# The order of VectorE's work per expert tile in a dense expert stage, and of the first tile loads on the SyncE queue

## What is computed

```python
def peer_ffn(x, w_q, sub_keys, u_tab, v_tab):
    ...
    best_s, pos = lax.top_k(cand_s, PEER_TOPK)
    expert = jnp.take_along_axis(cand_i, pos, axis=-1)
    gate = jax.nn.softmax(best_s, axis=-1).astype(x.dtype)
    ...
    def eval_block(args):
        xc, ec, gc = args
        u = u_tab[ec]
        act = jax.nn.gelu(jnp.einsum('cd,chkd->chk', xc, u), approximate=False)
        return jnp.einsum('chk,chkd->cd', act * gc, v_tab[ec])
```

## Time and profile before

| | |
|---|---|
| median of 3 runs | 1670.76 us (1669.7 to 1673.65) |
| the profiled execution | 1677.62 us, its span 1675.4 us |
| PE busy | 1625.1 us, 97% of the span |
| DVE busy | 1323.9 us, 79% |
| ACT, POOL busy | 703.8 us (42%), 594.1 us (35%) |
| first dense iteration | 864 us from the span's start |
| change from n < 64 to n >= 64 | about 1397 us |

### The profile page before, as it was taken

The page is one execution under the profiler, slowest core; times in us unless marked ns, Lnnn a source line. Parts: engine busy times, 40 slices in busy tenths (PEclk is TensorE's granted clock), DMA queues, the critical chain, the costliest instruction groups (busy, mean ns, idle before and its releaser), DMA issues.

```text
span 1675.4 us, 28110 instructions
## 1 busy us (share of the span) xinstructions
PE 1625.1 (97%) x10843; PEld 1440.7 (86%) x10843; DVE 1323.9 (79%) x2700; ACT 703.8 (42%) x1065; POOL 594.1 (35%) x400
## 2 busy tenths in 40 slices
PE   8999999999999997999999999999999999999997
PEld 7876579887889997999999999989989898788886
DVE  5657676883999998998836668888798889998777
ACT  4234542343333334888943333333333333333334
POOL 3100054103567751000012236556566565542110
PEclk9999999999999998999999999999999999999999
DMA  7331010132243452566498799999999999999994
GB/s 259 101 99 52 1 53 4 52 115 96 98 140 126 131 168 85 198 237 255 180 350 312 241 328 349 343 340 350 374 364 343 344 363 346 411 412 359 328 313 159
DMA packets 130724, 384.51 MB, mean 229 GB/s; under 512 B 12704, under 2 KB 53920, under 8 KB 129568
## 3 DMA queue, kind: packets, MB, share of 16 engines
q1 hardware_dynamic: 83216, 210.18, 35.7%
q0 software_dynamic: 37728, 159.40, 25.5%
q10 hardware_dynamic: 9648, 13.14, 2.2%
HBM read 340.73 MB, written 39.85 MB: 227 GB/s over the span
## 4 chain that ended last, share of the span: by engine, by line
PE 36%; DMA 10%; DVE 6%; POOL 4%; issue 3%; ACT 1%; SPq 0%; DVEq 0%; ACTq 0%
PE ps L192 11%; PE ps L193 10%; PE ps L194 10%; DMA u_selected<-in_u_rows,expert_index 8%; PE ps L2332 5%; POOL v_selected L2086 3%; POOL u_selected L2077 2%; DVE h L2234 1%; DMA mixed<-hidden_ahead 1%; DMA wq_raw<-in_u_t 1%; DVE dot_products L2221 1%; DVE v_lo L2267 1%; DVE a_lo L2270 1%; DVE hidden L2263 1%; DVE u_lo L2203 0%
## 5 line engine op out<-in xcount | busy, mean ns | idle before, releaser
L192 PE MATMUL ps<-v_hi,a_hi 128*128 128x512 f32 x768 | 299.8, 390 | 5.8 <-DVE a_lo L2270 5.5
L194 PE MATMUL ps<-v_hi,a_lo 128*128 128x512 f32 x768 | 298.8, 389 | 0.0
L193 PE MATMUL ps<-v_lo,a_hi 128*128 128x512 f32 x768 | 298.8, 389 | 0.0
L2086 POOL DMA_INDIRECT v_selected<-in_v,expert_index x128 | 186.9, 1460 | 280.6 <-DVE h L2234 262.8
L192 PE MATMUL ps<-xn_hi,u_hi 128*128 128x384 f32 (+1 forms) x768 | 262.0, 341 | 8.1 <-DVE xn_lo L1500 3.7
L194 PE MATMUL ps<-xn_hi,u_lo 128*128 128x384 f32 (+1 forms) x768 | 259.3, 338 | 0.0
L193 PE MATMUL ps<-xn_lo,u_hi 128*128 128x384 f32 (+1 forms) x768 | 259.2, 338 | 0.0
L2077 POOL DMA_INDIRECT u_selected<-in_u_rows,expert_index x128 | 176.7, 1380 | 153.1 <-DVE hidden_selected L2221 123.2
L2267 DVE TENSOR_TENSOR v_lo<-wout_raw,v_hi 128x1024 fp32r<-128x1024 f32 x128 | 156.3, 1221 | 64.8 <-ACT v_hi L2175 64.2
L2175 ACT ACTIVATE v_hi<-wout_raw 128x1024 fp32r<-128x1024 f32 x128 | 135.2, 1057 | 146.2 <-PE ps L194 143.5
L2221 DVE CUSTOM_DVE_ANT_0 dot_products<-u_selected,xn_tok 128x1024 bf16<-128x1024 f32 x128 | 154.3, 1219 | 45.1 <-DMA u_selected<-in_u_rows,expert_index 45.0
(11 more groups left out here) (333 smaller groups left out, 2975.0 us busy)
## 6 DMA issues: line engine op xcount, KB each, us to landing
wq_raw<-in_u_t SPq DMA_DIRECT2D x128, 512.0 KB
wout_raw<-in_v SPq DMA_DIRECT2D x128, 512.0 KB
gate_matrix<-gate_stage POOLq DMA_DIRECT2D x6, 4096.0 KB, 13.8
gates<-gate_matrix SPq DMA_DIRECT2D x32, 768.0 KB
win_raw<-in_win_t SPq DMA_DIRECT2D x25, 512.0 KB, 4.0
mixed<-hidden_ahead SPq DMA_DIRECT2D x64, 192.0 KB
wq_raw<-in_wq_t SPq DMA_DIRECT2D x16, 512.0 KB
hidden_ahead<-hidden_route ACTq DMA_DIRECT2D x34, 192.0 KB, 2.4
```

Of the source, the lines that this page charges most:

```text
L192: nc.tensor.matmul(out, w_hi, m_hi, start=first, stop=False)
L193: nc.tensor.matmul(out, w_hi, m_lo, start=False, stop=False)
L194: return nc.tensor.matmul(out, w_lo, m_hi, start=False, stop=last)
L2086: pool.indirect_dma_start(v_sel[:, k % GB, :], None, v_rows, bass.IndirectOffsetOnAxis(S.expert[:, k:k + 1], 0)).then_inc(s_vsel[k % GB], 16)
```

## The change

In DVE's dense iteration the gating of tile n now stands first, then the low part of the next U tile, then `v_lo` and `a_lo`, and only then the dot products and the combines. On SP the first three V tiles, which were asked for together right after U tile 30, are asked for one each after U tiles 31, 32 and 33. ACT's gelu of a batch of 16 dot products is put two steps later in its program.

```diff
@@ sync
             for m in range(NSTEP // 2 + UR, NMID + UR):
                 load_u(m)
-                if m == NMID:
-                    for n in range(VR - 1):
-                        load_v(n)
+                if m > NMID:
+                    load_v(m - NMID - 1)
@@ scalar
-                while dots < NSEL // BATCH and steps_before(n + 1) >= BATCH * (dots + 1) + 2:
+                while dots < NSEL // BATCH and steps_before(n + 1) >= BATCH * (dots + 1) + 4:
@@ vector
             for n in range(NKEY):
                 p = n % 2
-                if n < NLATE:
-                    split_u(NMID + n + 1)
                 some = range(steps_before(n), steps_before(n + 1))
-                for i in some:
-                    if i < NSEL:
-                        dot(i)
                 if n < NLATE:
                     dve.wait_ge(s_gelu, NMID + n + 1)
                     hidden = act_g[:, p, :]
...
                 v.tensor_tensor(act_g[:, p, :].rearrange("p (s t) -> p s t", t=SW),
                                 hidden.rearrange("p (s t) -> p s t", t=SW), gates[:, g % GR, :, n % GN, :],
                                 ALU.mult).then_inc(s_gated, 1)
+                if n < NLATE:
+                    split_u(NMID + n + 1)
                 dve.wait_ge(s_vhi, n + 1)
...
                                 ALU.subtract).then_inc(s_alo, 1)
+                for i in some:
+                    if i < NSEL:
+                        dot(i)
                 for i in some:
                     if i >= LAG:
                         combine(i - LAG)
```

## The result

Timed in turn on one chip, 22 executions each, the changed kernel takes 1673.6 us (1670.78 to 1677.69) and the kernel before 1669.86 us (1665.81 to 1673.65): ratio 1.0024, 95% interval 1.0016 to 1.0032, or +4.0 us. The profiled execution of the changed kernel is 1670.78 us, its span 1668.6. That of before took 1677.62, but there PE reaches the first matmul of `hidden(30)`, with which the dense loop begins, 5.5 us later, ahead of anything that was changed. So I compare from there on, in three stretches: from ACT's gelu of tile 0 of the dense loop to that of tile 2 (the **start**), on to that of tile 63 (the **loop**), and on to PE's last matmul (the **last stretch**).

A forecast was written before the change was run, and what follows sets the result against it. PE, busy 98.96 of 100 us in the dense loop with DMA engines 96% busy, was taken as the bound. Terms +4.06 + 0.5 + 3 = +7.6 us on the median 1670.76 gave 1678.4, say 1678; range 1669 to 1686.

The forecast's parts named there:

- `u_lo` behind the gating: Dense iteration 0: tile 31's `u_lo` follows a gating waiting for gate values until 872.39, so PE resumes later, +4.06 us.
- the clock: After PE's longer stop at tile 31: more low-clock time, bounds +0 to +2.5 us, taken as +0.5.
- The rule weighed: Start loads: each DMA engine takes a queue's descriptors in ring order, so gate values cannot pass six tiles; +4.06 stays.
- The U tile sooner, V tiles later: Start loads: U tile 31 lands some 4 us sooner but waits in SBUF; later V tiles and ACT's later gelu cost 0.
- `u_lo` in the loop: Dense loop: the new order bears a gating 1.63 us late, where the old one bore 5.26.
- The loop: Dense loop, dot products last: four late gathers cost PE 2 us each, 8 against 5.0 lost before, +3 us.
- lateness W: Dense loop: how late a gather comes for its dot product; 4.0 us for an 11.78 us gather, PE stopping above about 1.9.
- Rival A: Dense loop heals: late gathers no longer reach PE and 5.0 us come back, about 0 in total, 1670.4 us; chance 0.21.
- Iterations from 64 on: Last 64 iterations: no `u_lo`, same DVE work in the same period, 0.
- Rival B: Start: gate values land before 869.1, so +0.76 instead of +4.06; 1666.5 us with the loop healed, 1674.5 without; chance 0.08.
- Rival C: Dense loop: lateness feeds itself as gathers bunch and take 12 us, 10 to 15 us more, 1687 us; chance 0.14.

The follow-up runs named there:

- e1: Changed kernel with the low part of U tile 31 alone put back ahead of the first gating: 1670.29 us, ratio 0.9995 to the kernel before.
- e5: e1 with the first gate load moved up behind U tile 32, ahead of U tile 33 and V tiles 1 and 2: 1667.05 us, ratio 0.9983.
- e8: Changed kernel with the low part of the U tile back at the head of every iteration, dot products still last: 1670.93 us, ratio 1.0012.
- e2: Kernel before with only the change's new order of the first V and U loads: 1671.19 us, ratio 1.0001.
- e17: e5 with 111 gather steps in the first 64 iterations, one in iteration 63, and none in the last two iterations: 1664.8 us, ratio 0.9973.
- e11: Changed kernel with the dot products between `u_lo` and `v_lo`: 1674.63 us, ratio 1.003.
- e4: Kernel before, unchanged in what it does, as a second profile and measure of noise: 1670.33 us, ratio 0.9996.
- e3: Changed kernel with the new order of loads on SP undone: 1674.55 us, ratio 1.0026.
- e6: Changed kernel with the first gate load moved up behind U tile 32, `u_lo` still behind the first gating: 1670.34 us, ratio 1.0006.
- e13: e5 with four buffers, not three, for the hidden values returning from DRAM: 1665.45 us, ratio 0.9973.
- e7: e2, with DVE's old order, and the first gate load moved up behind U tile 32: 1666.44 us, ratio 0.998.
- e12: e7 with DVE's new order, dot products behind `a_lo`, in the last 64 iterations alone: 1666.92 us, ratio 0.9983.
- e14: e5 with half of each V tile's columns not loaded from iteration 64 on: 1666.05 us, ratio 0.9976.
- e16: e7 with 112 gather steps in the first 64 iterations and 40 in the last 64: 1691.79 us, ratio 1.0131.
- e15: e5 with 112 gather steps, not 106, in the first 64 iterations and 40 in the last 64: 1672.08 us, ratio 1.0012.

## Why the prediction was off

The direction was right and the size was not: 1678 was forecast, +7.2 on the median, and +4.0 is what came. By its own steps:

1. *`u_lo` behind the gating, +4.06, and 2. the clock, +0.5.* The stop was right: it was to be 6.39 us and was 6.50. By PE's rows the start was to cost 4.56 and cost 25.14 - 20.97 = 4.17, all of it the longer stop (6.50 - 2.33); the clock took no more than before, so +0, the lower bound, was the value and not +0.5. The chain named there is the one in the rows. That the gate load takes as long as before was right too (12.5 us, and 12.85). e1 and e5 showed it by taking the two links away one after the other.
   The rule weighed there, in the Trainium skill's DMA: Bandwidth & Descriptors, section on queues, rings and completion order, agrees with the traces: in e8, which holds the landings, the gate values issued at 859.0 us landed at 871.4, and the V tile issued just ahead of them, at 858.4, landed at 869.5. They did not pass it. Putting three of the tiles behind them (e5) took the wait away.
3. *The U tile sooner, V tiles later, 0.* Right: ACT's wait is gone, and it earned nothing. That ACT's later gelu of the dot products costs 0 has no run to itself. What I did not see is that even without `u_lo` behind the gating (e2) the gate values would stop PE, at the first outputs.
4. *`u_lo` in the loop: PE bears 1.63 us less lateness.* Never called on. Gatings came at gelu's end; the only wait left is DVE's for gelu.
5. *The loop, +3.* **This is the step that failed**, in its sign: it measured -2.4 on the average of traces (-5.6 in the two first). The room of the tightest gather was read rightly, 7.8 us, and the least in the changed kernel's trace is 7.73. What was wrong is the lateness W. I let a gather of 11.78 us, seen in the old order, meet that room, W = 11.78 - 7.8 = 4.0, and priced four such meetings. In the new order no dot product of the changed kernel waited at all, and the tight gathers of e5 and e17 took at most 8.15 us, though others took up to 10.1 and 12.5. That the meeting goes away once the dot products stand behind the gating, wherever else they stand, is shown by e8 and e11; that it is because DVE no longer runs ahead of gelu and lets the gathers go at uneven times is argued. Rival A, "the loop heals", was right here and had 0.21; a mean wait of 2.1 us with nothing left of it was the better reading of the earlier trace rows.
   The gain was priced from one trace as well: 5.0 us of PE's waits, where e4 had 1.3 and e2 0.3 us of them.
6. *Iterations from 64 on, 0.* **Failed as well**, unnoticed, since it was dismissed in a sentence. The last stretch is 272.48 us on the mean of the eight traces with the new order throughout and the old number of steps (changed, e1, e3, e5, e6, e8, e11, e13), and 270.86 in the four with the old order throughout (before, e2, e4, e7): +1.6. Of this about 1.1 us is, as I read e12 and e14, the price of DVE's order there; the rest differs from trace to trace, and its cause stays open.

In sum: +4.2 - 2.4 + 1.6 = +3.4, and +4.0 was timed (2.7 to 5.3). That the total was not missed by the whole 5.4 us of part 5 is luck: part 6, which stands at 0 in the sum, pays for 1.6 of them. Rival B, gate values in time, was not the case; e5 and e7 show what it would have been worth. Rival C, lateness that feeds itself, is not what the new order does. The old order loses 21 us in its loop in e16, at 6% more steps (112 for 106), but whether lateness feeds itself there was not looked into. What stays open is why 107 or 108 gathers were out at the 64th gelu in different executions of the old order, and how the 1.6 us split exactly.

## What to carry to other kernels

Before an instruction is put behind another, ask what the other waits for the first time, not only in the steady loop: here the first gating waits for a load that is issued last, and one `u_lo` behind it cost 4.2 us, more than the 2.4 that 61 quiet iterations returned. Do not let the longest transfer of the old order meet the tightest place of the new one without a reason: read how long the transfers take that have the least room, and bound the sum from those as well as from the longest. A change that mostly removes waits that nobody paid for may still be worth having if the freed room is used: measure both orders with more work in that room (e15 and e16 part by 1.2%), and look at the places where the period changes.

## What the runs showed that was not expected

- Five traces of one order differ by up to 5.0 us in the same stretch (504.87 to 509.87 us), with waits for gathers of 30.5 to 45.0 us. With the new order and the same steps all agree to 0.01 us. A stretch in which late gathers reach PE is not repeatable, and one trace of it is no price.
- The old order has an edge: with 112 steps in place of 106 in the loop it loses 18.6 us more (525.43 against 506.87), while the engines' share, 0.96 from 1200 to 1300 us, is that of before. The share did not give this away; the least room of a gather (5.3 us for 6.6) does. The new order carries the same steps at 375 GB/s (1200 to 1300 us of e15) with 1.2 us of waits.
- The load of the first gate values took 12.5 and 12.85 us until its reader went on in two orders of issue, and 12.4 (e8) and 13.7 us (e5, with fewer tiles issued ahead of it) until it landed. What brought it sooner in e5 was its earlier issue.
